# A hybrid attention network on one core: the attention's software pipeline made one step deeper

## The chip, the cores and the metric

The kernel runs on one core of one Trainium2 chip. The metric is the device time of one execution in microseconds (us), over the whole program. TensorE's engine is called PE, its weight loads PEld, VectorE is DVE, ScalarE is ACT, GpSimd is POOL, and SyncE, which issues most loads, is SP.

## What is computed

Two layers work on 512 tokens of width 1024. Each layer normalizes, projects, runs two kinds of attention side by side, projects back, and then runs a feed-forward part with a width-3 convolution. All is float32; the large products are made of three single-pass products of split operands.

```python
for l in range(2):
    proj = rms_norm(x, attn_norm[l]) @ w_in[l]
    q_lat, kv_lat, k_rope, nsa_q, nsa_kv, gate_logits = split(proj)
    o_mla = mla_attention(...)      # 8 heads, causal softmax over 512 keys
    o_nsa = nsa_attention(...)      # 8 heads in 2 groups; branches: compressed, selected, window
    x = x + concat([o_mla, o_nsa]) @ w_out[l]
    x = x + conv_ffn(rms_norm(x, ffn_norm[l]), ...)   # width 2816
out = rms_norm(x, final_norm)
```

At this length the selected branch (16 blocks of 64 tokens, of 8 that exist) and the window branch (512 tokens) are both plain causal attention with keys and values of their own. The compressed branch attends to 31 summaries, made by a small network from the first pair of keys and values.

## The kernel before, in words

Every engine has its own hand-written program, and semaphores tie them. There is no scheduler: what an engine does next is the order in its own list, and a wait holds everything behind it in that list.

**The attention of a layer** is one loop over 48 units (`U`, line 71) and a few steps for the pipeline to drain. A unit is one block of 128 queries of a pair of heads in one branch. Four units make a group `g` (12 groups: 4 of MLA, 8 of the other kind), in the order of `ORDER = (2, 3, 0, 1)` (line 74): causal units of 3, 4, 1 and 2 key blocks. Units of 3 and 4 blocks are "big" (line 606): each head takes a bank of PSUM of its own; the small ones put both heads into one bank. A unit passes through these stations:

- `scores(u)` (line 1620, PE): the products of queries and keys. MLA units use plain float32 (L1630), the others two products (L1635, L1636).
- `row_max(u)` (line 1191, DVE): adds the causal mask, writes the negated scores from PSUM into the tile `probs` and takes the row maximum (L1197).
- `exps(u)` (line 868, ACT): the exponential in place, with its row sum (L873).
- `turn(u)` (line 1639, PE): transposes the probabilities block by block into PSUM (L1649).
- `evac_turn(u)` (line 876, ACT): copies the transposed blocks to the tiles `pts` in SBUF (L884 and L887 for the two heads of a big unit, L891 for a small one).
- `values(u)` (line 1678, PE): for two units at once (odd u), the products with the values (L1696).
- per group: `factors(g)` (line 1200, DVE; L1203 and L1208 or L1212) makes one over the row sums, `spread(g)` (line 1654, PE; L1663) transposes them, `copy_factors(g)` (line 1220, DVE; L1223) brings them back, `normalize(g)` (line 1225, DVE; L1230, for every second later group also L1234) multiplies the output, `evac_out(g)` (line 895, ACT; L898, the first four groups only) and `out_lo` (line 1236, DVE; L1238) split it for the projection that follows.

**The loops.** PE, ACT and DVE each run over a step `s`. Before the change `LAG = 4` and `T_LAG = 3` (lines 72 and 73). In step s PE does turn(s-3), spread, scores(s), and values(s-4) on odd s, in that order. ACT does evac_turn(s-3), then exps(s). DVE does copy_factors, row_max(s), factors, normalize. Into this are hung single pieces of work at fixed steps (lines 108 to 116): projections in steps 0 to 2, eight "items" (transposes of queries and keys, `ITEM_STEP`, with `item_hi` on ACT and `item_lo` on DVE), the hidden layer of the compression (`HID_STEP` 7, L1731), its GELU over DVE, POOL, ACT and DVE again (L1315, L700 to L709, L941, L1321 to L1325), the product that needs it (`KVC_STEP` 11, L1835), the scores of the compressed branch and their softmax (steps 14 to 26), and four splits of output weights (`WOUT_STEP` 32, 36, 40, 44; L570 on ACT, L577 on DVE a step later).

**Banks.** PSUM has eight banks. Scores and spread factors go round banks 0 to 2, transposed probabilities round banks 3 and 4, and from step 29 on 3 to 5. The helper `ring` (line 125) hands out the bank that was used longest ago and names its former user; PE waits until that user has been read: `scores_read` (line 1605) for the row maxima or the copy of the factors on DVE, `turn_read` (line 1613) for the copies on ACT. The outputs of the first five groups share bank 6, so `out_free` (line 1667) makes values wait until the group before is normalized.

**Buffers.** `probs` (line 268) holds three units. row_max(u) may write only when turn(u-3) is done (line 1194). `pts` (line 269) are two tiles, each of four blocks, one for the units of 3 and 4 blocks and one for those of 1 and 2.

**After the loop's units** (s >= 48) PE fills its time with the first three parts of the output projection (`FILL = 3`, lines 1792 to 1799). The first of them waits for all row maxima, because it writes banks 0 to 3.

Of the kernel before, what the change touches and what calls it, by code (L numbers as in the profile page):

```python
# [32 lines left out]
P = 128  # L33
# [35 lines left out]
U_MLA = (H // 2) * T  # L69
U_NSA = (H // 2) * 2 * T  # L70
U = U_MLA + U_NSA
LAG = 4
T_LAG = 3
ORDER = (2, 3, 0, 1)


# [48 lines left out]
def ring(uses, banks):  # L125

    table, last = {}, {}
    for use, allowed in uses:
# [8 lines left out]
              (turn_uses(s) if s < U else [])]  # L137
TURN_USES = [(use, (3, 4) if s <= PC_STEP[1] + 2 else (3, 4, 5) if s < U else (4, 5)) for s in range(T_LAG, U + LAG)
             for use in (turn_uses(s - T_LAG) if s < U + T_LAG else []) +
             ([("f", NG - 1)] if s == U + LAG - 1 else [])]  # L140
SCORE_BANK = ring(SCORE_USES, 3)
TURN_BANK = ring(TURN_USES, 3)
FAC_BANK = [(TURN_BANK if g == NG - 1 else SCORE_BANK)["f", g] for g in range(NG)]
LAST_TURN_ON_3 = [use for use, _ in TURN_USES if TURN_BANK[use][0] == 3][-1]


# [23 lines left out]
def at(s, l, n):  # L170

    return l * PER_LAYER[s.name] + (n + CREDIT.get(s.name, 0))
# [74 lines left out]
def hybrid_layers(nc, a, out):  # L247

    with ExitStack() as ctx:
        def sb(name, shape, dt=F32, scope=ctx):  # L250
            return scope.enter_context(nc.sbuf_tensor(name, shape, dt))
# [13 lines left out]
        w_hi = sb("w_hi", [P, SLOTS, 1024], F32R)  # L265
        w_lo = sb("w_lo", [P, SLOTS, 1024], F32R)

        probs = sb("probs", [P, 3, 2, S])
        pts = [sb(f"probs_t{n}", [P, 2, T, 2 * P]) for n in range(2)]
        ident = sb("ident", [P, P])  # L270
        causal = sb("causal", [P, S])
        table = sb("table", [P, S])
# [43 lines left out]
        silu = sb("silu", [P, 2, S], F32, ffn)  # L316
        ffn.close()

        kpe_r = pts[1][:, 0, :, 0:2 * ROPE].rearrange("p t (a b) -> p t a b", a=2)
        rows = pts[0][:, 0, :, :].rearrange("p a (b c) -> p (a b) c", c=P)  # L320
        hn = probs[:, 0:2, :, :].rearrange("p s a n -> p s (a n)")
        norm_g = probs[:, 2, :, :].rearrange("p a n -> p (a n)")
# [425 lines left out]
        def _(act):  # L748
# [30 lines left out]
            for l in range(L):  # L779
# [88 lines left out]
                def exps(u):  # L868
                    n = (unit(u)[0] + 1) * P
                    for h in range(2):  # L870
                        row = probs[:, u % 3, h, 0:n]
                        act.wait_ge(max_done, at(max_done, l, 2 * u + h + 1))
                        activate(row, row, ACT.Exp, scale=-1.0, bias=nmax[:, u % 4, h:h + 1],  # L873
                                 accum_out=rsum[:, u // T % 2, unit(u)[0], h:h + 1]).then_inc(exp_done, 1)
# [43 lines left out]

                for s in range(U + LAG + 2):
                    if s < len(STEP_PROJ):  # L920
                        for job in STEP_PROJ[s]:
                            evac_proj(*job)
                    if 0 <= s - T_LAG < U:
                        evac_turn(s - T_LAG)
                    if s < U:
                        exps(s)
                    if s == 2:
                        act.wait_ge(gate_in, at(gate_in, l, 1))
                        activate(gates[:, :, :], gate_e[:, :, :], ACT.Exp, scale=-1.0).then_inc(gate_exp, 1)
                    g = (s - LAG - 1) // T  # L930
                    if s > LAG and (s - LAG - 1) % T == T - 1:
                        if g < H // 2:
                            evac_out(g)
                    if s in ITEM_STEP:
                        item_hi(ITEM_STEP.index(s))
                    if s == HID_STEP:
                        act.wait_ge(cmp_used, at(cmp_used, l, 4))
                        activate(hid_rows, ps[:, HID_BANK, 0:CHID], ACT.Copy).then_inc(hid_out, 1)
                    if s == HIDT_STEP + 1:
                        act.wait_ge(gelu_in, at(gelu_in, l, 1))  # L940
                        activate(gelu_t, gelu_t, ACT.Exp, scale=-2.0 * (2.0 / np.pi) ** 0.5).then_inc(gelu_exp, 1)  # L941
                    if s == KVC_STEP:
                        act.wait_ge(kvc_acc, at(kvc_acc, l, 1))
                        activate(kc[:, :, :], ps[:, KVC_BANK, S - G * NCP:S].rearrange("p (g c) -> p g c", g=G), ACT.Copy)\
                            .then_inc(kch_done, 1)
                    if s in CS_STEP:
                        g = CS_STEP.index(s)
                        act.wait_ge(cs_acc, at(cs_acc, l, g + 1))
                        activate(cs_t[g], ps[:, CS_BANK[g], :], ACT.Copy).then_inc(cs_out, 1)
                    if s in CS_EXP_STEP:  # L950
                        g = CS_EXP_STEP.index(s)
                        act.wait_ge(cs_sub, at(cs_sub, l, g + 1))
                        activate(sc_flat[g], sc_flat[g], ACT.Exp).then_inc(cs_exp, 1)
                    if s in PC_STEP:
                        g = PC_STEP.index(s)
                        act.wait_ge(pc_tp, at(pc_tp, l, g + 1))
                        activate(pct[:, g, :], ps[:, PC_BANK, :], ACT.Copy).then_inc(pct_ready, 1)
                    if s in WOUT_STEP:
                        split_hi(act, l, POS_WOUT + WOUT_STEP.index(s))
# [82 lines left out]
        def _(dve):  # L1042
# [47 lines left out]
            for l in range(L):  # L1090
# [99 lines left out]

                def row_max(u):
                    n = (unit(u)[0] + 1) * P
                    if u >= 3:
                        dve.wait_ge(t_done, at(t_done, l, turns(u - 3, 1 if big(u - 3) else 0)))
                    for h in range(2):
                        dve.wait_ge(sc_done, at(sc_done, l, 2 * u + (h + 1 if big(u) else 2)))
                        v.tensor_tensor_reduce(probs[:, u % 3, h, 0:n], score_place(u, h), causal[:, S - n:S], -1.0, -NEG,  # L1197
                                               ALU.add, ALU.min, nmax[:, u % 4, h:h + 1]).then_inc(max_done, 1)

                def factors(g):  # L1200
# [85 lines left out]
                for s in range(U + LAG + 2):  # L1286
# [5 lines left out]
                        add_compressed((s - LAG - 1 - U_MLA) // (2 * T))  # L1292
                    if LAG <= s < U + LAG and (s - LAG) % T == T - 1:
                        copy_factors((s - LAG) // T)
                    if s < U:
                        row_max(s)
                    if s < len(STEP_PROJ):
                        for job in STEP_PROJ[s]:
                            evac_proj(*job)
                    if 0 <= s - 2 < U and (s - 2) % T == T - 1:  # L1300
                        factors((s - 2) // T)
                    if s > LAG and (s - LAG - 1) % T == T - 1:
                        normalize((s - LAG - 1) // T)
                    if closed and done >= H // 2 and done % 2 == 1:
# [143 lines left out]
        def _(pe):  # L1448
# [30 lines left out]
            for l in range(L):  # L1479
# [132 lines left out]

                def turn_read(use):

                    if use is not None and use[1] == 0:
                        pe.wait_ge(pt_act, at(pt_act, l, use[0] + 1))
                    elif use is not None:
                        pe.wait_ge(pt_second, at(pt_second, l, pt_second_count(use[0])))
# [20 lines left out]
                def turn(u):  # L1639
                    blocks = unit(u)[0] + 1  # L1640
                    for h in range(2):
                        pe.wait_ge(exp_done, at(exp_done, l, 2 * u + h + 1))
                        if h == 0 or big(u):
                            turn_read(TURN_BANK[u, h][1])
                        bank, c0 = (TURN_BANK[u, h][0], 0) if big(u) else (TURN_BANK[u, 0][0], h * blocks * P)
                        if bank == PC_BANK and TURN_BANK[u, h if big(u) else 0][1] is None:
                            pe.wait_ge(pct_ready, at(pct_ready, l, G))
                        for b in range(blocks):
                            last = nc.tensor.transpose(ps[:, bank, c0 + b * P:c0 + (b + 1) * P],  # L1649
                                                       probs[:, u % 3, h, b * P:(b + 1) * P], ident[:, :])  # L1650
                        if h == 1 or big(u):
                            last.then_inc(t_done, 1)

                def spread(g):

                    pe.wait_ge(fac_ready, at(fac_ready, l, g + 1))
                    bank, prev = FAC_BANK[g]
                    if g == NG - 1:
                        turn_read(prev)
                    else:  # L1660
                        scores_read(prev)
                    for i in range(T):
                        last = nc.tensor.transpose(ps[:, bank, i * P:(i + 1) * P], onorm[:, g % 2, i * P:(i + 1) * P],  # L1663
                                                   ident[:, :])
                    last.then_inc(fac_done, 1)
# [85 lines left out]
                for s in range(U + LAG):  # L1751
# [35 lines left out]
                        pe.wait_ge(k_ready, at(k_ready, l, H // 2))  # L1787
                    if s >= LAG + U_MLA and (s - LAG - U_MLA) % (2 * T) == 2 * T - 1:
                        compressed((s - LAG - U_MLA) // (2 * T))
                    if s >= LAG and s % 2 == 1:  # L1790
                        values(s - LAG)
                    if s >= U and s - U < FILL:
                        pe.wait_ge(max_done, at(max_done, l, 2 * U))
                        if s == U:
                            pe.wait_ge(fac_out, at(fac_out, l, NG - 1))
                            turn_read(LAST_TURN_ON_3)
                        pe.wait_ge(lo_done, split(l, POS_WOUT + s - U))
                        for t in range(2):
                            project_out(t, s - U, [ht_hi[:, s - U, :], ht_lo[:, s - U, :]], s == U, False)
                    if s == T_LAG:  # L1800
                        pe.wait_ge(q_ready, at(q_ready, l, H))
                    if s == ITEM_STEP[0]:
                        pe.wait_ge(q_roped, at(q_roped, l, 1))
# [197 lines left out]
```

## Time and profile before

| | us |
|---|---|
| median of 3 runs | 1308.6 (1306.14 to 1309.12) |
| the profiled execution | 1306.81 |
| its span, first to last instruction | 1305.0 |
| PE busy in the span | 1263.9 (97%) |
| DVE busy | 700.7 (54%) |
| ACT busy | 639.0 (49%) |
| POOL busy | 71.3 (5%) |
| mean granted TensorE clock | 0.997 |

The span leaves out 1.8 us that lie around it. The attention loop of layer 0 runs from about 101.7 us to 251.7 us of the span, that of layer 1 from about 744 to 894. A row of the timeline gives the start, the duration, the engine and line, the tiles written and read, and in brackets how long the engine sat idle before it and what ended that. A row of a waits view gives the waiting engine and line, the one that released it, the sum in us, the number of times and the longest. PE's rows overlap: a matmul's record lasts longer than the distance to the next one's start, so the cost of a piece of PE work is read from start to start.

### The profile page before, as it was taken

The numbers are of one execution on the slowest core, as the hardware profiler recorded it, in microseconds if no ns is written. First come the engines' busy times: TensorE is split into PE (matmuls) and PEld (weight loads), VectorE is DVE, ScalarE is ACT, GpSimd is POOL, SyncE is SP. The second block draws the span as 40 slices with busy tenths as digits, with TensorE's granted clock in tenths as the row PEclk, the third lists the DMA queues.
The fourth block names the chain that finished last, engine by engine and source line by source line (L and its number), as shares of the span: only waits on it lengthen the run. The fifth ranks groups of instructions, "written<-read, shape, count | busy, mean of one in ns | idle before, by whom it ended". The sixth has DMA issues, their size and how long they took to land.

```text
span 1305.0 us, 18503 instructions
## 1 busy us (share of the span) xinstructions
PE 1263.9 (97%) x6612; PEld 1044.6 (80%) x6612; DVE 700.7 (54%) x1226; ACT 639.0 (49%) x1193; POOL 71.3 (5%) x165
## 2 busy tenths in 40 slices
PE   8999989999999999999999998999999999999997
PEld 7997667778888888888889866767888888888886
DVE  5435788454555555533363458872555555554334
ACT  4436789344444444322352468882454444443223
POOL 2003120000000000000010311100000000000000
PEclk9999999999999999999999999999999999999999
DMA  6420101124333333322143210022223333333211
GB/s 206 125 89 1 66 2 49 50 67 126 96 96 97 96 95 98 110 95 96 44 122 95 65 66 1 2 66 81 81 77 97 96 96 97 96 102 111 96 64 65
DMA packets 121003, 107.05 MB, mean 82 GB/s; under 512 B 3763, under 2 KB 110485, under 8 KB 120946
## 3 DMA queue, kind: packets, MB, share of 16 engines
q1 hardware_dynamic: 118912, 101.13, 25.2%
q0 software_dynamic: 1456, 3.52, 0.9%
q10 hardware_dynamic: 578, 1.64, 0.3%
q8 instruction: 35, 0.57, 0.2%
q14 instruction: 22, 0.18, 0.0%
HBM read 104.19 MB, written 2.10 MB: 81 GB/s over the span
## 4 chain that ended last, share of the span: by engine, by line
PE 84%; DVE 9%; ACT 4%; issue 2%; DMA 1%; POOL 0%; DVEq 0%; ACTq 0%; POOLq 0%
PE ps L1453 24%; PE ps L1455 24%; PE ps L1454 24%; PE ps L1649 3%; PE ps L1696 3%; DVE probs L1197 2%; PE ps L1630 2%; ACT probs L873 1%; DVE probs L1070 1%; DVE w_lo L577 1%; PE ps L1636 1%; PE ps L1635 1%; DVE x L1088 1%; PE ps L1708 1%; PE ps L1663 1%
## 5 line engine op out<-in xcount | busy, mean ns | idle before, releaser
L1453 PE MATMUL ps<-ht_hi,w_hi 128*128 128x512 f32 (+2 forms) x776 | 298.0, 384 | 2.5 <-DVE w_lo L577 2.5
L1454 PE MATMUL ps<-ht_lo,w_hi 128*128 128x512 f32 (+2 forms) x776 | 296.4, 382 | 0.0
L1455 PE MATMUL ps<-ht_hi,w_lo 128*128 128x512 f32 (+2 forms) x776 | 296.4, 382 | 0.0
L577 DVE TENSOR_TENSOR w_lo<-raw,w_hi 128x1024 fp32r<-128x1024 f32 (+4 forms) x196 | 218.6, 1140 | 95.9 <-ACT w_hi L570 86.3
L570 ACT ACTIVATE w_hi<-raw 128x1024 fp32r<-128x1024 f32 (+4 forms) x196 | 187.2, 983 | 108.3 <-PE ps L1455 107.1
L1369 DVE SCALAR_TENSOR_TENSOR conv<-ps,cols,conv 128x510 f32<-128x510 f32 (+1 forms) x176 | 127.6, 745 | 181.5 <-ACT conv L982 175.6
L1453 PEld LDWEIGHTS ps<-ht_hi,w_hi 128*128 128x128 f32 x776 | 146.4, 189 | 30.9 <-DVE w_lo L577 2.9
L1454 PEld LDWEIGHTS ps<-ht_lo,w_hi 128*128 128x128 f32 x776 | 146.4, 189 | 28.2 <-issue 0.5
L1455 PEld LDWEIGHTS ps<-ht_hi,w_lo 128*128 128x128 f32 x776 | 146.3, 189 | 27.7
L1453 PE MATMUL ps<-w_hi,ht_hi 128*128 128x430 f32 (+1 forms) x392 | 147.0, 375 | 3.3 <-DVE w_lo L577 2.0
L982 ACT ACTIVATE conv<-ps,cols 128x512 f32<-128x512 f32 x88 | 68.1, 774 | 160.0 <-PE ps L1455 159.7
L1455 PE MATMUL ps<-w_hi,ht_lo 128*128 128x430 f32 (+1 forms) x392 | 144.2, 368 | 0.0
L1454 PE MATMUL ps<-w_lo,ht_hi 128*128 128x430 f32 (+1 forms) x392 | 144.2, 368 | 0.0
L1453 PE MATMUL ps<-w_hi,g_hi 128*128 128x512 f32 x352 | 137.2, 390 | 0.8 <-DVE g_all L1377 0.8
L1454 PE MATMUL ps<-w_lo,g_hi 128*128 128x512 f32 x352 | 137.0, 389 | 0.0
L1455 PE MATMUL ps<-w_hi,g_lo 128*128 128x512 f32 x352 | 136.9, 389 | 0.0
L873 ACT ACTIVATE probs<-probs,nmax 128x384 f32<-128x384 f32 (+1 forms) x192 | 106.2, 557 | 30.2 <-DVE nmax L1197 29.7
L1197 DVE CUSTOM_DVE_ANT_0 probs<-ps,causal 128x384 f32<-128x384 f32 (+1 forms) x192 | 86.8, 486 | 42.7 <-PE ps L1630 22.5
L1001 ACT ACTIVATE g_hi<-g_all 128x512 fp32r (+1 forms) x44 | 27.6, 630 | 149.8 <-PE ps L1455 149.8
L1390 DVE TENSOR_TENSOR g_lo<-g_all,g_hi 128x512 fp32r<-128x512 f32 x44 | 30.2, 691 | 129.8 <-ACT g_hi L1001 129.8
L1649 PE MATMUL ps<-ident,probs 128*128 128x128 f32 x480 | 72.1, 278 | 17.7 <-ACT probs_t L891 9.7
L1453 PEld LDWEIGHTS ps<-w_hi,ht_hi 128*128 128x128 f32 x392 | 73.8, 188 | 11.7 <-DVE w_lo L577 2.6
(201 smaller groups left out, 1506.4 us busy)
## 6 DMA issues: line engine op xcount, KB each, us to landing
raw<-in_ffn_w_up_dram SPq DMA_DIRECT2D x88, 512.0 KB, 4.2
raw<-in_ffn_w_down_dram SPq DMA_DIRECT2D x44, 512.0 KB, 3.3
raw<-in_w_in_dram SPq DMA_DIRECT2D x32, 430.0 KB, 4.2
raw<-in_w_out_dram SPq DMA_DIRECT2D x16, 512.0 KB, 3.3
raw<-in_nsa_cmp_w_dram SPq DMA_DIRECT2D x8, 512.0 KB, 3.6
x<-in_x_dram ACTq DMA_DIRECT2D x3, 512.0 KB, 8.2
raw<-in_mla_w_uq_dram SPq DMA_DIRECT2D x4, 384.0 KB, 3.0
out_dram<-x SPq DMA_DIRECT2D x3, 512.0 KB, 2.6
```

Source lines behind the costliest of these rows:

```text
L570: last = nc.scalar.activation(d(w_hi)[:, :, d0:d1], r(raw)[:, :, r0:r1], ACT.Copy)
L577: last = nc.vector.tensor_tensor(d(w_lo)[:, :, d0:d1], r(raw)[:, :, r0:r1], d(w_hi)[:, :, d0:d1].bitcast(F32), ALU.subtract)
L873: activate(row, row, ACT.Exp, scale=-1.0, bias=nmax[:, u % 4, h:h + 1], accum_out=rsum[:, u // T % 2, unit(u)[0], h:h + 1]).then_inc(exp_d ...
L982: activate(conv[:, fl, uv, :], ps[:, 4 * fl + uv, :], ACT.Identity, bias=bias, scale=tap)\
L1197: v.tensor_tensor_reduce(probs[:, u % 3, h, 0:n], score_place(u, h), causal[:, S - n:S], -1.0, -NEG, ALU.add, ALU.min, nmax[:, u % 4, h:h ...
L1369: ins = stt(out=conv[:, fl, uv, back:S], in0=ps[:, 4 * fl + uv, 0:S - back], scalar=c, in1=conv[:, fl, uv, back:S], op0=ALU.mult, op1=ALU.add)
L1390: tt(g_lo[:, n % 2, :].unsqueeze(1), g_all[:, bass.ds(k, 1), :], g_hi[:, n % 2, :].unsqueeze(1).bitcast(F32), ALU.subtract).then_inc(gl_do ...
L1453: mm(o, lhs[0], rhs[0], start=start, stop=False)
L1454: mm(o, lhs[0], rhs[1], start=False, stop=False)
L1455: return mm(o, lhs[1], rhs[0], start=False, stop=stop)
L1649: last = nc.tensor.transpose(ps[:, bank, c0 + b * P:c0 + (b + 1) * P], probs[:, u % 3, h, b * P:(b + 1) * P], ident[:, :])
L1696: last = mm(ps[64 * h:64 * h + VD, out_bank(g), q0 + q:q0 + 2 * P], w, pt_half(u)[:, h, b, q:2 * P], start=b == 0, stop=b == n - 1)
```

## The change

`LAG` becomes 5 and `T_LAG` 4. `probs` gets a fourth buffer; the second tile of `pts`, which serves the units of 1 and 2 blocks only, shrinks to two blocks. In step s PE now does turn(s-4), spread, scores(s), and values(s-5) on even s. ACT does evac_turn(s-4) and then exps(s-1). On DVE `factors` moves from one step after the group's last exponentials were issued to the head of the step behind, ahead of row_max; copy_factors and normalize follow one step later than before. The single pieces of work stay at their steps. The spread of group 10 falls to step 48, so that it takes a bank of the transposes' ring. The wait for all queries goes from step `T_LAG` to the first item's step, which is again step 3.

```diff
-LAG = 4
-T_LAG = 3
+LAG = 5
+T_LAG = 4
...
-             ([("f", NG - 1)] if s == U + LAG - 1 else [])]
+             ([("f", (s - LAG) // T)] if s >= U and (s - LAG) % T == T - 1 else [])]
...
-FAC_BANK = [(TURN_BANK if g == NG - 1 else SCORE_BANK)["f", g] for g in range(NG)]
+FAC_BANK = [(SCORE_BANK if ("f", g) in SCORE_BANK else TURN_BANK)["f", g] for g in range(NG)]
...
-        probs = sb("probs", [P, 3, 2, S])
-        pts = [sb(f"probs_t{n}", [P, 2, T, 2 * P]) for n in range(2)]
+        probs = sb("probs", [P, 4, 2, S])
+        pts = [sb(f"probs_t{n}", [P, 2, T // (n + 1), 2 * P]) for n in range(2)]
...
-                        row = probs[:, u % 3, h, 0:n]
+                        row = probs[:, u % 4, h, 0:n]
...
-                    if s < U:
-                        exps(s)
+                    if 1 <= s <= U:
+                        exps(s - 1)
...
-                    if u >= 3:
-                        dve.wait_ge(t_done, at(t_done, l, turns(u - 3, 1 if big(u - 3) else 0)))
+                    if u >= 4:
+                        dve.wait_ge(t_done, at(t_done, l, turns(u - 4, 1 if big(u - 4) else 0)))
...
+                    if 0 <= s - 3 < U and (s - 3) % T == T - 1:
+                        factors((s - 3) // T)
                     if s < U:
                         row_max(s)
...
-                    if 0 <= s - 2 < U and (s - 2) % T == T - 1:
-                        factors((s - 2) // T)
...
-                    if use is not None and use[1] == 0:
+                    if use is not None and use[0] == "f":
+                        pe.wait_ge(fac_out, at(fac_out, l, use[1] + 1))
+                    elif use is not None and use[1] == 0:
...
-                    if g == NG - 1:
+                    if ("f", g) not in SCORE_BANK:
...
-                    if s >= LAG and s % 2 == 1:
+                    if s >= LAG and (s - LAG) % 2 == 1:
                         values(s - LAG)
...
-                            pe.wait_ge(fac_out, at(fac_out, l, NG - 1))
+                            pe.wait_ge(fac_out, at(fac_out, l, sum(("f", g) in SCORE_BANK for g in range(NG))))
...
-                    if s == T_LAG:
+                    if s == ITEM_STEP[0]:
                         pe.wait_ge(q_ready, at(q_ready, l, H))
```

## Rows read from the trace of the kernel before

**Rows 1.** The page's first part: busy time of each engine, share, instructions.
```profile
PE 1263.9 (97%) x6612; PEld 1044.6 (80%) x6612; DVE 700.7 (54%) x1226; ACT 639.0 (49%) x1193; POOL 71.3 (5%) x165
```

**Rows 2.** Windows: the two attention loops; length, busy time by engine, PE clock.
```profile
113.40:251.70 138.30, 127.62 (x968) 94.70 (x967) 98.29 (x290) 102.76 (x295) 12.83 (x17) 1.00 0.09 32
...
755.90:894.30 138.40, 127.74 (x968) 94.80 (x967) 98.34 (x290) 102.80 (x295) 12.88 (x17) 1.00 0.09 32
```

**Rows 3.** Waits of PE in the attention loop of layer 0, 113.4 to 251.7.
```profile
PE ps L1649 <- ACT probs_t L891: 4.8, 3, 2.4
PE ps L1649 <- ACT probs_t L884: 4.0, 5, 1.4
PE ps L1747 <- DVE ks L1249: 1.3, 1, 1.3
PE ps L1851 <- DVE qs L1251: 0.5, 1, 0.5
```

**Rows 4.** Waits of ACT in the same stretch: the exponentials.
```profile
ACT probs L873 <- DVE nmax L1197: 14.9, 21, 1.4
```

**Rows 5.** Timeline of PE: the longest wait of the late groups, turn(45).
```profile
234.89 1.06 PE L1649 MATMUL ps<-ident,probs 128*128 128x128 f32 x8 [1.39 <-ACT probs_t L884]
```

**Rows 6.** Timeline of PEld: the weight load ahead of the same wait.
```profile
234.86 0.85 PEld L1649 LDWEIGHTS ps<-ident,probs 128*128 128x128 f32 x8 [1.60 <-ACT probs L873]
```

**Rows 7.** Timeline of ACT at the start of the loop of layer 0.
```profile
105.18 1.28 ACT L873 ACT_TABLE_LOAD   x1
106.48 0.62 ACT L873 ACTIVATE probs<-probs,nmax 128x384 f32<-128x384 f32 x1
...
108.33 1.20 ACT L850 ACTIVATE km<-ps 64x512 f32<-64x512 f32 x2 [0.54 <-PE ps L1455]
```

**Rows 8.** Timelines of ACT, DVE and POOL, layer 0, steps 8 to 11.
```profile
134.93 0.61 ACT L898 ACTIVATE ht_hi<-onorm 128x512 fp32r<-128x512 f32 x1
...
138.16 0.47 DVE L1315 TENSOR_SCALAR hid<-ps,hid_b 128x62 f32<-128x62 f32 x2
...
139.55 1.39 DVE L1249 TENSOR_TENSOR ks<-ps,ks 64x512 fp32r<-64x512 f32 x2
...
140.46 0.54 POOL L709 TENSOR_SCALAR tmp_pool<-tmp_pool 128x128 f32<-128x128 f32 x1 [0.20 <-POOL tmp_pool L705]
...
142.34 0.95 DVE L1323 RECIPROCAL tmp_pool<-tmp_pool 128x128 f32<-128x128 f32 x1
...
143.33 0.29 DVE L1325 TENSOR_TENSOR hid<-hid,tmp_pool 128x128 f32<-128x128 f32 x1
```

**Rows 9.** Timeline of DVE in steps 45 and 46 of layer 0.
```profile
229.38 0.68 DVE L1197 CUSTOM_DVE_ANT_0 probs<-ps,causal 128x512 f32<-128x512 f32 x1
...
230.83 0.69 DVE L1212 TENSOR_TENSOR onorm<-fac,gates 128x512 f32<-128x512 f32 x1
...
232.04 1.22 DVE L577 TENSOR_TENSOR w_lo<-raw,w_hi 128x1024 fp32r<-128x1024 f32 x1
...
233.17 0.28 DVE L1197 CUSTOM_DVE_ANT_0 probs<-ps,causal 128x128 f32<-128x128 f32 x1
```

**Rows 10.** Timeline of PE: an MLA step, then one whole later group.
```profile
133.78 1.88 PE L1630 MATMUL ps<-km,qm 128*128 128x512 f32 x4
135.59 1.74 PE L1696 MATMUL ps<-probs_t,vm 128*64 128x256 f32 x16
...
196.01 0.84 PE L1649 MATMUL ps<-ident,probs 128*128 128x128 f32 x6
...
197.78 0.87 PE L1696 MATMUL ps<-probs_t,proj 128*64 128x256 f32 x8
198.58 1.09 PE L1649 MATMUL ps<-ident,probs 128*128 128x128 f32 x8
199.43 0.42 PE L1635 MATMUL ps<-ks,qs 128*128 128x384 f32 x1
...
204.02 0.84 PE L1649 MATMUL ps<-ident,probs 128*128 128x128 f32 x6
```

More of the change, by code:

```diff
@@ L317, in hybrid_layers @@
         ffn.close()
-        kpe_r = pts[1][:, 0, :, 0:2 * ROPE].rearrange("p t (a b) -> p t a b", a=2)
+        kpe_r = pts[1].rearrange("p a t c -> p (a t) c")[:, :, 0:2 * ROPE].rearrange("p t (a b) -> p t a b", a=2)
         rows = pts[0][:, 0, :, :].rearrange("p a (b c) -> p (a b) c", c=P)
@@ L1192, in row_max @@
                     n = (unit(u)[0] + 1) * P
-                    if u >= 3:
-                        dve.wait_ge(t_done, at(t_done, l, turns(u - 3, 1 if big(u - 3) else 0)))
+                    if u >= 4:
+                        dve.wait_ge(t_done, at(t_done, l, turns(u - 4, 1 if big(u - 4) else 0)))
                     for h in range(2):
                         dve.wait_ge(sc_done, at(sc_done, l, 2 * u + (h + 1 if big(u) else 2)))
-                        v.tensor_tensor_reduce(probs[:, u % 3, h, 0:n], score_place(u, h), causal[:, S - n:S], -1.0, -NEG,
+                        v.tensor_tensor_reduce(probs[:, u % 4, h, 0:n], score_place(u, h), causal[:, S - n:S], -1.0, -NEG,
                                                ALU.add, ALU.min, nmax[:, u % 4, h:h + 1]).then_inc(max_done, 1)
@@ L1649, in turn @@
                             last = nc.tensor.transpose(ps[:, bank, c0 + b * P:c0 + (b + 1) * P],
-                                                       probs[:, u % 3, h, b * P:(b + 1) * P], ident[:, :])
+                                                       probs[:, u % 4, h, b * P:(b + 1) * P], ident[:, :])
                         if h == 1 or big(u):
```

## The prediction, made before the changed kernel was run

> **What bounds the kernel now.** I began with the page's busy times: PE has work for 97% of the span [rows 1], so the whole time stands at most some tens of us above PE's own work. A change to the attention's order adds and removes no PE instruction, so it can only win or lose PE's waiting. The windows of the two attention loops say how much that is: 138.3 us with 127.62 busy, and 138.4 with 127.74 [rows 2], about 10.7 us idle in each. ACT is busy for 103 us there and DVE for 98, so neither is the bound over a whole loop, but a group can be. The waits view names what ended the idle time: 8.8 us by ACT's copies of transposed blocks (L891, L884), in 8 waits, and 1.8 by DVE, in two [rows 3]. The timeline shows the longest late one at turn(45), 1.39 us [rows 5]; its weight load waited 1.60 [rows 6], so each wait also costs 0.21 us of drain that still counts as busy. The ten waits are thus worth 10.6 + 10 x 0.21 = 12.7 us a layer, 25 us in all: the most that the change can win. Layer 1 shows the same ten.
>
> Why are ACT's copies late? In ACT's list evac_turn stands behind the exponentials of the step before, and these wait for a fresh row maximum: 14.9 us a layer in 21 waits for DVE [rows 4]. The deeper pipeline lets exps(s-1) run on maxima that are a step old. That wait should go almost wholly, and PE's eight waits for copies with it.
>
> **What is added, part by part.** Nothing is added in instructions: the same copies, exponentials, transposes and products, and no DMA (SP's loads hang on other steps; POOL's load after the loop waits for the last transpose, but stands behind its last copy, which comes later anyway). The fourth `probs` buffer is free of cost: no wait in the trace is for the old three. One more drain step has no work of its own; the copies of turn(47) are covered by spread and the compressed product. What costs is order. I follow each list through steps 3 to 52, one layer, with durations of the rows, a hand-over from PE to DVE of 0.3 and from ACT or DVE to PE of 0.1 to 0.15 us.
>
> *The start.* exps(0) moves behind the keys' copy of step 1, which ended at 109.53, and takes its table load (1.28) along [rows 7]; before, the load fell into idle time. From there ACT works without a gap (exps 0 to 2, keys, gates, item 0) and copies turn(0) at 117.2; its half is done at 117.64, and PE, which reaches turn(1) at 116.8, waits 1.0. In this case the load ends at 106.46 and the exponential starts at 106.48, with nothing behind it [rows 7], so I add nothing. The Trainium skill (ScalarE: Activation LUTs, "What ACT_TABLE_LOAD costs") puts a drain of about 1.38 us on top of each load; by it this wait would be 2.4 us and the whole 2.8 us slower than my sum. The trace speaks against it.
>
> *values behind normalize.* For groups 1 to 4 values wait until the group before is normalized. normalize used to follow a 3-block row_max; now it follows the 4-block one of step 4g+5, and values come on the next step, after just a 1-block turn and scores. In MLA, from scores(9)'s start: scores take 1.81 [rows 10], the second maximum starts 0.3 later and takes 0.69, normalize 0.69, ready for PE at 3.6; PE is there at 1.81 + 0.45 (item) + 0.22 + 0.45 = 2.9. Wait 0.5 to 0.6 for groups 1 and 2. In groups 3 and 4 the scores are shorter and no item covers: 0.8 and 1.1. Together 3.0.
>
> *GELU before KVC_STEP.* This is the largest. Count from the start of turn(5). scores(9) end at 2.7, normalize(0) at 4.4, DVE's hidden-layer pieces (L1315) at 5.1. ACT does evac_out (0.61) at 4.5 and item 2 (1.19) to 6.3. DVE does out_lo, factors and row_max(10) to 6.8 and item_lo(2), 1.39, to 8.2; then the GELU's three instructions, 0.94 + 0.95 + 0.29 with gaps, 2.25, to 10.4 [rows 8]. PE, without turn(8), spread(1) and values(7), which used to stand ahead of it, gets to KVC_STEP at 8.0. Wait 2.5, in place of the 2.4 [rows 3] that this same chain costs now through POOL (L709 [rows 8]) and ACT.
>
> *Scores behind a busy DVE.* Three banks and seven uses a group: the second half of scores(4k) now takes the bank of scores(4k-1), the step before, and needs its maximum. DVE's list in between, from the 4-block maximum: 1.21, normalize 0.69, in every second group a sum of the same shape (0.69), the weight split 1.13 (232.04 to 233.17), factors 0.85, the 1-block maximum 0.42, out_lo 0.6, the 2-block maximum 0.76: 6.4 us [rows 9]. It starts 0.8 behind scores(37). PE from there to the second half of scores(40): the group's 8.01 less values 0.80, turn 0.85 and half the 3-block scores 0.35, thus 6.0 [rows 10]. 0.8 + 6.4 + 0.15 - 6.0 = 1.3 wait at step 40. Without the sum and out_lo the list is 5.1 and fits; without the split (step 32) 0.2. At step 48 the same list holds back the output projection, which needs all maxima, and spread(10) needs a copy of turn(44) at once: 0.65. Together 2.2.
>
> *The rest*, found in the same way: item 6 behind item_lo(5) 0.4, turn(14) behind item 7 on ACT 0.3, turn(20) 0.7 and scores(24) 0.5 around the compressed softmax, turn(24) 0.15. Together 2.1.
>
> **The sum.** Added per layer 1.0 + 3.0 + 2.5 + 2.2 + 2.1 = 10.8; removed 12.7. Gain 1.9 a layer, 3.8 in all; I take 3.6, for small hand-overs. The profiled execution took 1306.81, so 1303.2; the median of the runs is 1.8 above it, so against that 1305.0. Bounds of the unknown waits: if the GELU chain and normalize are hidden by what PE does ahead of them, 2.5 + 3.0 less half, so 3 a layer, are not paid, gain 10. If each of the 14 new waits is 0.3 longer than worked out (as much as one hand-over to DVE), 4.2 a layer more are lost.
>
> **Rivals.** *The covers hold*: ACT's slack removes the waits and the new ones are half of mine; for it speaks that the removed 14.9 us of ACT's waiting [rows 4] exceed all of PE's. 1308.6 - 10 = 1298.6. *Nothing to be measured*: old and new waits cancel within 0.2%, about what a measurement of this kernel can tell from no change (2.6 us). The banks for transposes (two, later three) and scores (three) stay, and all of PE's waits for ACT are for a bank [rows 3]; only the `probs` buffer grows, which no wait names. If the bubbles are set by banks, the time stays 1308.6. The Trainium skill (Perfetto Trace Analysis, "Optimization Strategy") says that a gap that repeats on the engine that should be full can mean too little SBUF or PSUM for the next tile; by that rule this change gives room in the memory that isn't short. *Slower, by DVE*: the place is the step after the 4-block maximum, where normalize, split and factors now pile up (4.0 us between two maxima [rows 9], where factors, out_lo and split stood before), with PE waiting for it in values, KVC, items and scores(4k). It decides from the point where the added waits exceed 12.7 a layer, that is with 0.15 us more on each of 14. At 0.3 more each: (4.2 - 1.9) x 2 = 4.6 slower, 1313.2. Against it: I counted ready times from records of the same instructions.
>
> **How the numbers follow.** Forecast, a small gain around 1305.0: 0.42. Covers hold, 1298.6: 0.13. Nothing, 1308.6: 0.2. Slower by DVE, 1313: 0.25. Of the forecast 0.35 and of the covers all lies below 1306.0, so faster 0.48; same 0.07 + 0.2 = 0.27; slower 0.25. Both signs hold much of the chance: the forecast's own range is 1302 to 1308. The range for 8 in 10 reaches to both other cases, 1298 to 1313.
>
> **What would show it.** Right: PE's waits for L884 and L891 fall from 8.8 us a layer to under 3; ACT's wait for L1197 from 14.9 to under 4; new are a wait of 2 to 3 us at L1835 for L1325, waits at L1696 for L1230 in four groups, and at step 40 one at L1635 for L1197. Wrong: waits of L1649 for ACT still near 8 us (banks decide), or no wait at L1835, or waits for DVE above 11 us a layer. A granted clock under 1.00 in the loop would be outside all of this.

## The result, and the profile after

| | before | changed |
|---|---|---|
| median | 1307.49 us (6 runs) | 1315.71 us (6 runs, 1314.57 to 1317.45) |
| ratio | | 1.0063, 95% interval 1.0052 to 1.0073: slower |
| profiled execution | 1306.81, span 1305.0 | 1317.45, span 1315.6 |
| mean granted clock | 0.997 | 0.993 |

The forecast was 1305.0 with a range of 1298 to 1313. The change made the kernel slower where a gain was forecast, and the time lies outside the range. (The rows of after have the line numbers of the changed kernel: of the lines in PE's program that the text names, all but L1453 to L1455 are two higher.)

The page's first part answers to [rows 1]. PE was busy for 7.4 us longer, with the same 6612 instructions:

```profile
PE 1271.3 (97%) x6612; PEld 1050.5 (80%) x6612; DVE 704.6 (54%) x1226; ACT 638.3 (49%) x1193; POOL 78.3 (6%) x165
```

Next, windows from the first product of scores to the start of the last values, first in the kernel before, then in the changed one. Columns: the window, its length, busy time (and records) of PE, PEld, DVE, ACT, POOL, then the granted clock, the DMA share and GB/s.

```profile
101.69:248.17 146.48, 135.80 (x997) 100.65 (x995) 102.79 (x306) 111.04 (x311) 20.76 (x51) 1.00 0.09 30
744.24:890.70 146.46, 135.80 (x997) 100.66 (x995) 102.78 (x306) 111.02 (x311) 20.75 (x51) 1.00 0.09 30
```
```profile
102.03:254.16 152.13, 140.42 (x997) 104.26 (x995) 104.69 (x306) 110.67 (x311) 24.26 (x51) 0.98 0.08 29
750.67:902.82 152.15, 140.46 (x996) 104.27 (x994) 104.70 (x306) 110.67 (x311) 24.25 (x51) 0.98 0.09 29
...
143.40:146.80 3.40, 3.40 (x17) 2.79 (x14) 1.92 (x3) 2.85 (x12) 0.00 (x0) 0.52 0.00 0
...
239.00:242.40 3.40, 3.40 (x13) 2.54 (x10) 1.81 (x4) 0.17 (x2) 0.00 (x0) 0.52 0.02 7
791.90:795.30 3.40, 3.40 (x24) 2.81 (x13) 2.04 (x3) 2.98 (x12) 0.00 (x0) 0.53 0.00 0
887.50:890.90 3.40, 3.40 (x15) 2.42 (x12) 1.94 (x4) 0.30 (x2) 0.00 (x0) 0.53 0.00 0
```

Each loop is 5.65 to 5.69 us longer, and this is where the time went. Idle time (length less busy) rose only from 10.7 to 11.7. Busy time rose by 4.6, and the last four windows say why: twice in each loop the clock falls to half (1.2 in place of 2.4 GHz) for 3.4 us (the windows lie up to 0.2 us beside these stretches, so that they read 0.52 or 0.53). Before, the only such stretch ahead of the program's last few us was in the feed-forward part of layer 1 (936.2 to 939.6), and after the change that one is gone. The span's 10.6 us more are 11.3 in the loops, 0.3 ahead of the first, 0.4 between them, and 1.5 less behind the second (414.3 to 412.8).

The waits of PE from 100 to 250, layer 0, which answer to [rows 3], and ACT's wait, which answers to [rows 4]. Columns: who waits, for whom, us in total, times, the longest.

```profile
PE ps L1837 <- DVE hid L1325: 2.6, 1, 2.6
PE ps L1698 <- DVE onorm L1230: 2.6, 4, 1.1
PE ps L1637 <- DVE nmax L1197: 2.1, 3, 1.1
PE ps L1665 <- ACT probs_t L884: 2.0, 1, 2.0
PE ps L1651 <- ACT probs_t L884: 0.9, 2, 0.7
PE ps L1665 <- DVE onorm L1212: 0.6, 1, 0.6
PE ps L1720 <- DVE qs L1251: 0.5, 1, 0.5
PE ps L1651 <- ACT probs_t L891: 0.2, 1, 0.2
```
```profile
ACT probs L873 <- DVE nmax L1197: 3.5, 5, 1.3
```

ACT's 14.9 us of waiting for maxima fell to 3.5, as it should, and PE's waits for copies from 8.8 to 3.1. In their place stand waits for DVE, 8.4 us in ten where there had been 1.8 in two. All in all there are 14 waits, 11.5 us, where ten with 10.6 us had been. The two longest, on PE's timeline (start, duration, idle time before in brackets), and the matmuls behind the second:

```profile
142.66 0.41 PE L1837 MATMUL ps<-hid,cmp_w 128*128 128x64 f32 x2 [2.65 <-DVE hid L1325]
...
237.96 0.63 PE L1665 MATMUL ps<-ident,onorm 128*128 128x128 f32 x4 [2.02 <-ACT probs_t L884]
...
240.45 0.63 PE L1455 MATMUL ps<-w_hi,ht_lo 128*128 128x512 f32 x1
240.88 0.63 PE L1453 MATMUL ps<-w_hi,ht_hi 128*128 128x512 f32 x1
...
243.27 0.40 PE L1454 MATMUL ps<-w_lo,ht_hi 128*128 128x512 f32 x1
243.51 0.39 PE L1455 MATMUL ps<-w_hi,ht_lo 128*128 128x512 f32 x1
```

Each of the two is followed by one of the windows at half clock, in which products start 0.43 apart (240.45 to 240.88) in place of 0.24. Why is the second 2.02 long? DVE and ACT ahead of it:

```profile
232.69 0.69 DVE L1230 TENSOR_TENSOR onorm<-ps,onorm 128x512 f32<-128x512 f32 x1
233.48 0.69 DVE L1234 TENSOR_TENSOR onorm<-onorm 128x512 f32<-128x512 f32 x1
234.09 1.22 DVE L577 TENSOR_TENSOR w_lo<-raw,w_hi 128x1024 fp32r<-128x1024 f32 x1
...
235.45 0.87 DVE L1212 TENSOR_TENSOR onorm<-fac,gates 128x512 f32<-128x512 f32 x1
236.24 0.28 DVE L1197 CUSTOM_DVE_ANT_0 probs<-ps,causal 128x128 f32<-128x128 f32 x1
```
```profile
236.56 0.40 ACT L873 ACTIVATE probs<-probs,nmax 128x128 f32<-128x128 f32 x1 [1.29 <-DVE nmax L1197]
...
237.35 0.47 ACT L884 ACTIVATE probs_t<-ps 128x384 f32<-128x384 f32 x1
```

The pile of [rows 9] is there in its new order: maxima, normalize, sum, split, factors, maxima. exps(46) waits 1.29 for it, the copy of turn(44) stands behind exps(46) in ACT's list, and PE waits for the copy.

### The profile page after: what moved, and what is told of

The parts are those of the page before. It is cut to its first block, busy times and chain, and to the rows that moved or that the text cites. A ratio compares the mean times of both kernels' runs of the same rounds, so it can differ in the third digit from the quotient of the medians.

```text
span 1315.6 us, 18499 instructions
## 1 busy us (share of the span) xinstructions
PE 1271.3 (97%) x6612; PEld 1050.5 (80%) x6612; DVE 704.6 (54%) x1226; ACT 638.3 (49%) x1193; POOL 78.3 (6%) x165
## 4 chain that ended last, share of the span: by engine, by line
PE 86%; DVE 8%; ACT 3%; issue 2%; DMA 1%; POOL 1%; DVEq 0%; ACTq 0%; POOLq 0%
PE ps L1453 24%; PE ps L1454 24%; PE ps L1455 24%; PE ps L1651 3%; PE ps L1698 3%; PE ps L1632 2%; DVE probs L1197 1%; PE ps L1637 1%; PE ps L1638 1%; DVE w_lo L577 1%; DVE probs L1070 1%; DVE x L1088 1%; PE ps L1665 1%; DVE onorm L1230 1%; PE ps L1710 1%
## 5 line engine op out<-in xcount | busy, mean ns | idle before, releaser
L1453 PE MATMUL ps<-ht_hi,w_hi 128*128 128x512 f32 (+2 forms) x776 | 297.5, 383 | 2.5 <-DVE w_lo L577 2.5
L1455 PE MATMUL ps<-ht_hi,w_lo 128*128 128x512 f32 (+2 forms) x776 | 296.2, 382 | 0.0
L1453 PEld LDWEIGHTS ps<-ht_hi,w_hi 128*128 128x128 f32 x776 | 145.9, 188 | 30.9 <-DVE w_lo L577 2.9
L1455 PEld LDWEIGHTS ps<-ht_hi,w_lo 128*128 128x128 f32 x776 | 145.9, 188 | 28.0
L1454 PEld LDWEIGHTS ps<-ht_lo,w_hi 128*128 128x128 f32 x776 | 146.0, 188 | 27.7 <-issue 0.5
L1453 PE MATMUL ps<-w_hi,ht_hi 128*128 128x430 f32 (+1 forms) x392 | 148.5, 379 | 4.4 <-DVE ht_lo L1077 2.4
L1455 PE MATMUL ps<-w_hi,ht_lo 128*128 128x430 f32 (+1 forms) x392 | 145.4, 371 | 0.0
L1453 PE MATMUL ps<-w_hi,g_hi 128*128 128x512 f32 x352 | 137.3, 390 | 0.8 <-DVE g_all L1377 0.8
L1455 PE MATMUL ps<-w_hi,g_lo 128*128 128x512 f32 x352 | 137.1, 390 | 0.0
L1453 PEld LDWEIGHTS ps<-w_hi,ht_hi 128*128 128x128 f32 x392 | 74.7, 190 | 13.7 <-DVE ht_lo L1077 2.9
L1455 PEld LDWEIGHTS ps<-w_hi,ht_lo 128*128 128x128 f32 x392 | 74.4, 190 | 7.2
```

What stands on the lines that cost most here:

```text
L1453: mm(o, lhs[0], rhs[0], start=start, stop=False)
L1454: mm(o, lhs[0], rhs[1], start=False, stop=False)
L1455: return mm(o, lhs[1], rhs[0], start=False, stop=stop)
```

## Experiments

The theory: DVE's order makes PE's new waits, and the two long ones also cost clock. Twelve kernels bear on it. The table has every run: its ratio to the kernel before, the lengths of the two loops (first scores to last values), and the number of 3.4 us stretches at half clock in each (one of 6.8 counts as two). The last column is the first loop less 1.73 us for each such stretch: about the loop's length by its waits alone (where that price comes from, and that it can be up to 0.25 too high for a stretch, is under a4_split). Medians are of all executions of a kernel, loops and stretches those of the profiled one, and executions of one kernel differ in clock: a2_norm's profiled one took 1303.2 at a mean clock of 0.992, its other three 1298.5 to 1299.3 at 0.996 to 0.997.

| run | median | ratio (95% interval) | loops | half clock | at full clock |
|---|---|---|---|---|---|
| before | 1307.49 | 1 | 146.5 / 146.5 | 0 / 0 | 146.5 |
| changed | 1315.71 | 1.0063 (1.0052 to 1.0073) | 152.1 / 152.2 | 2 / 2 | 148.7 |
| a1_fill | 1320.70 | 1.0094 (1.0069 to 1.0118) | 153.2 / 153.2 | 0 / 0 | 153.2 |
| a2_norm | 1298.93 | 0.9927 (0.9903 to 0.9951) | 145.1 / 145.2 | 2 / 2 | 141.7 |
| a3_kvc | 1320.22 | 1.0089 (1.0064 to 1.0113) | 152.6 / 151.1 | 2 / 1 | 149.2 |
| a4_split | 1306.30 | 0.9988 (0.9976 to 1.0000) | 147.8 / 146.0 | 1 / 0 | 146.0 |
| a5_fill | 1312.81 | 1.0033 (1.0021 to 1.0044) | 149.4 / 149.3 | 0 / 0 | 149.4 |
| b1_exps | 1303.18 | 0.9956 (0.9943 to 0.9969) | 144.9 / 143.3 | 1 / 0 | 143.2 |
| c1_both | 1300.16 | 0.9934 (0.9921 to 0.9946) | 144.9 / 143.4 | 2 / 1 | 141.4 |
| c2_more | 1301.66 | 0.9950 (0.9939 to 0.9962) | 144.8 / 144.8 | 1 / 1 | 143.0 |
| d1_lag | 1331.15 | 1.0179 (1.0165 to 1.0192) | 159.3 / 159.0 | 3 / 3 | 154.1 |
| d2_hid | 1296.84 | 0.9909 (0.9895 to 0.9922) | 143.0 / 141.3 | 1 / 0 | 141.3 |
| d3_b1norm | 1295.22 | 0.9900 (0.9887 to 0.9914) | 141.1 / 141.1 | 0 / 0 | 141.1 |
| d4_warm | 1297.97 | 0.9914 (0.9899 to 0.9930) | 141.8 / 141.8 | 0 / 0 | 141.8 |

**The clock (a1_fill, a5_fill).** Dummy transposes ahead of the two long waits, once what they write may be written:

```diff
+                        turn_read(TURN_BANK[8, 0][1])
+                        junk(24)          # a1_fill: 44
                         pe.wait_ge(it_act, at(it_act, l, 3))
...
+                        turn_read(LAST_TURN_ON_3)
+                        junk(18)          # a1_fill: 36
```

> The changed kernel with TensorE kept at work in its two longest waits of a layer: 44 transposes of the identity into a bank that is free, just ahead of the product at KVC_STEP, and 36 ahead of spread(10). They add nothing to the result. Clock theory: the granted clock falls to half after these two waits, for 3.4 us each time, four times in all, and each costs some 1.6 us; then the clock stays at full speed in the loops, and the time falls by 5 to 7 us, to about 1309 to 1311. Rival, the waits alone make the loss and the low clock costs nothing since other engines are late anyway: time within 1 us of the changed kernel's 1315.7, whatever the clock does.

The half-clock stretches in the loops went, but each transpose takes 0.112 us: the 44 outlast the wait of 2.65 by some 2.3 us, the 36 theirs by 2. The time rose, which neither side had forecast, and it says nothing about the theory's sum. Sized to the waits:

> The changed kernel with 24 dummy transposes ahead of TensorE's wait for the hidden layer (2.65 us) and 18 ahead of its wait at the step 48 copy (2.02 us); at 0.112 us each they take 2.7 and 2.0 us, as long as the waits. Theory (each of these waits is followed by 3.4 us at half the clock, 1.7 us lost a time): the work arrives when it did, no stretch at half clock is left in the two loops, and the time is 5 to 7 us less than the changed kernel's 1315.7: 1309 to 1311. Rival (the clock costs nothing on the path, the queues behind make it up): within 1 us of 1315.7.

Measured 1312.8, some 3 us below the changed kernel (4 by the ratios): neither forecast. The loops lost 2.77 and 2.82 us. Counted from the first loop's start, the product at KVC_STEP came 0.5 later (41.13 in place of 40.63), since the filling could start only 0.46 after PE was there. From it to spread(10) PE gained 1.73 (93.57 in place of 95.30), from there to the last values 1.54 (14.66 in place of 16.20). One stretch appeared at 942.6 in the feed-forward part (some 1.6 us), where the changed kernel had none. So the clock is on the path: its two stretches cost 1.73 and 1.54, 3.3 us a layer. That the place of a stretch can shift out of the loop I had not counted.

**DVE's order (a2_norm, a4_split, c1_both).** normalize ahead of the step's maxima; the weight splits two steps later; both.

```diff
+                    if s > LAG and (s - LAG - 1) % T == T - 1:
+                        normalize((s - LAG - 1) // T)
                     if 0 <= s - 3 < U and (s - 3) % T == T - 1:
...
-                    if s > LAG and (s - LAG - 1) % T == T - 1:
-                        normalize((s - LAG - 1) // T)
...
-                    if s - 1 in WOUT_STEP:
-                        split_lo(dve, l, POS_WOUT + WOUT_STEP.index(s - 1))
+                    if s - 3 in WOUT_STEP:
+                        split_lo(dve, l, POS_WOUT + WOUT_STEP.index(s - 3))
```

> The changed kernel with normalize moved ahead of row_max in DVE's list, within the same step. Order theory: DVE had to pass the 4-block maximum before it could normalize, and values waited for it; the waits of L1698 for L1230 (2.6 us a layer and 0.2 of drain for each of four) go, the GELU chain starts 0.7 us earlier, and DVE's list before the last maxima is 0.7 to 1.4 us shorter: the time falls by 6 to 10 us, to 1306 to 1310. Rival, DVE is simply full and its order matters little: what values gain, row_max and scores lose, less than 2 us.

> The changed kernel with DVE's four splits of output weights two steps later, behind the 2-block maximum in place of the 4-block one. Order theory: the list between the 4-block and the 2-block maximum is 1.13 us shorter, so the waits at step 40 (0.60 and 0.67) go and the wait for turn(44)'s copy at step 48 (2.02) falls to about 0.9, and with it the low clock behind it: 2 x (1.3 + 1.1) to 2 x (1.3 + 1.1 + 1.6), 5 to 8 us less, 1308 to 1311. Rival, these waits hang on ACT's load alone: unchanged, within 1.5 us of 1315.7.

a2_norm, 1298.9, is faster than the kernel before, and 7 us under the best that its theory forecast. Its waits of PE, 100 to 250:

```profile
PE ps L1837 <- DVE hid L1325: 2.3, 1, 2.3
PE ps L1637 <- DVE nmax L1197: 1.3, 1, 1.3
PE ps L1651 <- ACT probs_t L884: 0.9, 2, 0.7
PE ps L1665 <- ACT probs_t L884: 0.6, 1, 0.6
PE ps L1651 <- ACT probs_t L891: 0.6, 1, 0.6
PE ps L1720 <- DVE qs L1251: 0.4, 1, 0.4
```

The four waits for normalize are gone, and with them those for maxima at steps 32 and 40, and 1.4 of the 2.02 at spread(10): 11.5 became 6.1. normalize had stood behind factors and the step's two maxima, and PE behind normalize. The loops are 7.0 us shorter with as many half-clock stretches as in the changed kernel: 5.4 of idle time, and seven waits fewer, of 0.21 of drain each.

a4_split, 1306.3, beat its theory's 1308 to 1311 too, and it gives the clock's price. Its two loops have the same waits (9.5 us against 9.4), and its windows:

```profile
102.07:249.83 147.76, 138.20 (x997) 102.88 (x995) 104.47 (x306) 110.35 (x311) 23.74 (x51) 0.99 0.09 30
745.87:891.90 146.03, 136.50 (x996) 101.88 (x994) 104.44 (x306) 110.36 (x311) 23.73 (x51) 1.00 0.09 30
143.80:147.20 3.40, 3.40 (x13) 2.33 (x11) 2.02 (x4) 2.40 (x11) 0.00 (x0) 0.53 0.00 0
```

The first loop has one stretch at half clock, the second none: 1.73 us. Of the other runs in which the two loops differ by one stretch, d2_hid gives 1.71, b1_exps 1.60, c1_both 1.52 and a3_kvc 1.48, so the price is 1.5 to 1.7. The Trainium skill (TensorE: Matmul & The Clock Gate, "HAM oscillation — how this bites in real kernels") charges throttled time with one half of its length. That is 1.7 for 3.4, and the traces agree for the dearest stretches; the cheapest cost 0.2 less. The wait at spread(10) fell from 2.02 to 0.7, and no half clock followed it.

> The changed kernel with two orders on VectorE: a group's normalisation ahead of the step's maxima, and the weight splits two steps later. Theory (the waits for the normalisation and for the copy at step 48 are separate orders of VectorE's queue, and their effects add): waits behind the normalisation none, at the step 48 copy under 0.7, time 1293 to 1297. Rival (they are one and the same backlog, seen twice): no better than the first alone, 1298 to 1300.

The rival held: 1300.2 is no better than a2_norm, and at full clock the loop is 141.4 against 141.7. The wait at spread(10) stayed 0.6. It was one backlog, seen at two places.

**The wait for the hidden layer (a3_kvc, c2_more, d2_hid, d4_warm).** First, PE asks a step later (KVC_STEP 12; DVE's reader of that bank moved to the head of its step).

> The changed kernel with the product that needs the GELU (KVC_STEP) at step 12 in place of 11 and DVE's copy of it at the head of step 13. Order theory: the wait of 2.65 us falls under 0.7, the low clock behind it goes with it: (2 + 1.6) x 2 = about 7 us less, 1309. Rival, DVE's queue of item_lo and GELU sets the end there, and the wait moves to items or transposes behind it: less than 3 us gained.

The rival held. The wait at KVC_STEP is gone, and PE waits 2.6 at turn(8) instead. The time even rose, to 1320.2: half clock came up in both feed-forward parts (from 301.3 and from 949.8), and went in one place of the loops only. Waits of PE, 100 to 250:

```profile
PE ps L1651 <- ACT probs_t L891: 3.4, 3, 2.6
```

ACT's copy stands behind ACT's own step in the GELU (L941), which waits for POOL: 1.71 us, here and in the changed kernel. Asking later does not help an engine whose next wait is for the same queue. Second, on top of c1_both, the hidden layer's pieces (L1315) at the head of DVE's step 9, in c2_more with the compressed scaling one step later too (`CS_SCALE_STEP` 23, 25).

> As the one before, and the hidden layer's pieces of VectorE at the head of its step 9, and the compressed cache's scaling a few steps later. Theory: TensorE's wait for the hidden layer falls from 2.3 to about 0.5 us, that for the maxima from 1.3 to under 0.5, and with them both stretches at half clock of each layer go: 1284 to 1292. Rival (the wait moves to the copies and maxima that now stand behind the pieces, as it did when the step was only put later): within 2 us of the run before.

> The run with both orders on VectorE, and VectorE's work on the hidden layer at the head of its step 9, but the compressed cache's scaling where it was. Theory (the late scaling is what made the two new waits for GpSimd's operands, 1.9 and 1.2 us, in the run that had both): those two waits are gone, the wait for the hidden layer is 1.7 us and that for the maxima 1.3 as before, and the time is 1297 to 1300. Rival (the earlier hidden layer itself pushes the operands back): the two waits stay, 1301 to 1303.

c2_more was no better than c1_both (within the rival's 2 us): the wait for the hidden layer fell to 1.7 and that for maxima went, but two came in. Waits of PE in c2_more, 100 to 256:

```profile
PE ps L1870 <- POOL v_operand L731: 1.9, 1, 1.9
...
PE ps L1870 <- POOL k_operand L731: 1.2, 1, 1.2
```

d2_hid without the late scaling has neither, at 1296.8. Its gain over c1_both is clock: at full clock the loops are alike (141.3 and 141.4), but it has one half-clock stretch where c1_both has three. Third, c1_both with 20 dummy transposes (2.2 us) in the wait of 2.3:

> The run with both orders on VectorE, and 20 dummy transposes (2.2 us at 0.112 us each) ahead of TensorE's wait for the hidden layer (2.3 us). Theory (the wait costs its own length and 1.73 us of clock behind it): the first stretch at half clock of each layer goes and the time falls by 2 x 1.7 us to 1296 to 1297.5. Rival (the clock falls anyway behind the later wait of 1.3 us, or in the next stage): 1299 or more.

1298.0, between the two. All three stretches of the loops went, the second of layer 0 too, though the wait of 1.3 us ahead of it was still there. One came up at 289.9 in the feed-forward part; the loops fell by 3.0 and 1.5, and 1.6 was given back there.

**The parts of the change (b1_exps, d1_lag, d3_b1norm).** b1_exps is the kernel before with one edit, d1_lag the changed kernel with the same edit undone:

```diff
-                    if s < U:
-                        exps(s)
+                    if 1 <= s <= U:
+                        exps(s - 1)
```

(The fourth buffer is no part of b1_exps.) d3_b1norm is b1_exps with DVE's two orders.

> The kernel before with one part of the change alone: the exponentials of a step issued behind the copies of that step, factors and values where they were, three buffers. Theory (this shift is the useful part: ScalarE's 14.9 us of waits for maxima a layer go, and with them the copies' lateness; the one-step shift of the values is what put the normalisations behind VectorE's long step): 1297 to 1303. Rival (the exponentials come too late for turns that were not moved, so TensorE waits there instead): 1307 or more.

> The changed kernel with one part undone: the exponentials of a step again behind the copies of that same step, the rest (fourth buffer, turns, values and factors a step later) as changed. Theory (the exponentials' shift is what took ScalarE's waits for maxima away; the deeper pipeline alone only moves the values behind VectorE's long step): ScalarE waits again some 10 to 15 us a layer for maxima, TensorE's waits for copies come back in part, and the waits for the normalisation stay: 1316 to 1324, slower than the changed kernel or equal to it. Rival (the turns, one step later, no longer feel a late exponential, and the exponentials' shift is what makes the copies late): faster than the changed kernel, 1308 to 1313.

Both theories held in their signs, the first at the edge of its range, the second beyond it: 1331.2 where 1316 to 1324 was forecast, with 24.0 us of ACT's waiting for maxima where it was 10 to 15. The exponentials' shift alone gives 1303.2: ACT has no wait for maxima left from 100 to 250, and PE's waits for copies are 3.9 us. The rest of the change alone (turns, values and factors moved, one more buffer) gives 1331.2, some 23 us slower than before; which of these parts costs how much was not tried. The waits in d1_lag, 101 to 262 (the last row: ACT, 100 to 256):

```profile
PE ps L1651 <- ACT probs_t L891: 6.3, 3, 2.6
PE ps L1837 <- DVE hid L1325: 2.9, 1, 2.9
PE ps L1651 <- ACT probs_t L884: 2.1, 3, 1.0
PE ps L1698 <- DVE onorm L1230: 1.9, 3, 1.1
PE ps L1698 <- ACT probs_t L884: 1.5, 2, 0.8
```
```profile
ACT probs L873 <- DVE nmax L1197: 24.0, 25, 2.8
```

PE's waits for copies are at the level of before (8.4 for the turns), and the waits for DVE came on top.

> The kernel before with the exponentials' shift and the same two orders on VectorE as in the run with both, so without the one-step shift of turns, values and factors. Theory (the deeper pipeline is worth what it takes from the waits for copies, some 1 to 2 us a layer, once nothing on VectorE is in its way): 1301 to 1303, slower than the same orders on the deeper pipeline (1300). Rival (the deeper pipeline gives nothing at all): 1297 to 1299.

The rival held, and more: 1295.2 is the fastest of all, 1% under the kernel before, with clock 0.999. Once DVE's order is right, the deeper pipeline buys nothing: without it the loops are 141.1 and 141.1, and those of c1_both at full clock 141.4 and 141.6. c1_both's two loops are 6.0 us longer together, and its three stretches are some 5 of that. Waits of PE in d3_b1norm, 100 to 256:

```profile
PE ps L1649 <- ACT probs_t L891: 2.4, 2, 1.5
PE ps L1747 <- DVE ks L1249: 0.9, 1, 0.9
PE ps L1635 <- DVE nmax L1197: 0.8, 2, 0.4
PE ps L1649 <- ACT probs_t L884: 0.7, 2, 0.6
PE ps L1708 <- ACT vm L957: 0.2, 1, 0.2
```

The orders of DVE without the exponentials' shift were not tried on the kernel before.

## Why the prediction was wrong

**What bounds the kernel** held: PE's waits, 25 us in all, and nothing else to win; the best kernel won 13 of them. **What the change removes** held in part. ACT's wait for maxima fell to 3.5 (forecast: under 4), PE's waits for copies to 3.1 (under 3, so just missed). These 3.1 are waits that the sum had among the added ones: 0.74 at turn(1), 0.41 at turn(14) and turn(20), and 2.02 ahead of spread(10).

**The added waits** were found at their places; only turn(24) showed none. Per layer, forecast and idle time measured: start and turn(1) 1.0 and 0.7; values behind normalize 3.0 and 2.6; KVC_STEP 2.5 and 2.65; scores at steps 32 and 40 1.5 and 1.65; the rest 2.1 and 2.0; step 48 0.65 and 2.02. Two terms of the sum failed:

- *Step 48, sized 1.4 too small.* "spread(10) needs a copy of turn(44) at once" was priced by the pile of DVE alone. The copy stands behind exps(46) on ACT, and exps(46) behind the pile: DVE's lateness was handed on through ACT's list. The text named the pile and the copy, and never put them in one chain.
- *The drain.* The old waits were credited with 0.21 each on top of the idle time, the new ones were not charged it. Like with like it is 11.5 + 14 x 0.21 = 14.4 against 12.7: waits alone cost 1.7 us a layer where I gained 1.9.

One term came out right by luck. The GELU's three instructions were priced 0.94 + 0.95 + 0.29, as in [rows 8], and took 0.23 + 0.95 + 1.11. The last one ran beside a cast on POOL:

```profile
141.30 1.11 DVE L1325 TENSOR_TENSOR hid<-hid,tmp_pool 128x128 f32<-128x128 f32 x1
```
```profile
140.10 2.17 POOL L717 CAST ks<-ks 64x1024 fp32r<-64x1024 f32 x2 [0.42 <-DVE ks L1249]
```

The forecast never asked what POOL does beside DVE. The 0.8 us that L1325 took longer lie in PE's wait of 2.65.

**The clock** is the step that failed altogether. The sum took each wait at its own length; "a granted clock under 1.00 in the loop would be outside all of this" named it and gave it no price and no chance. Two stretches a layer cost 3.3 of the 5.65 us (a5_fill). What causes the remaining 0.6 (5.65 less 1.7 and 3.3) is not shown. Forecast and result differ by 7.5 us a layer in the loops: 3.6 by waits, 3.3 by clock, 0.6 by the rest; the kernel before's own stretch, gone in the feed-forward part, gave 1.5 back once. With the waits counted right and no loss of clock the change would have come out some 4 us slower; with the clock it left the range.

**The rivals.** *Slower, by DVE* (1313.2, chance 0.25) is what happened, with its place, its turning point of 12.7 a layer and nearly its price in waits (14.4; it had 15.0); the clock made up the difference. *Nothing, since banks decide*, did not hold: with no bank added, PE's waits for copies fell by more than half in b1_exps (8.8 to 3.9) and in the changed kernel. The Trainium skill (Perfetto Trace Analysis, "Optimization Strategy") says of repeated gaps that they can mean too little SBUF or PSUM. That was not so here: order in two queues made these gaps. *The covers hold* did not happen; only a part of the change, b1_exps, made the kernel faster. *The table load:* turn(1) waited 0.74, not 2.4, and in the changed kernel too the load's end at 111.17 is 0.01 ahead of the exponential:

```profile
109.89 1.28 ACT L873 ACT_TABLE_LOAD   x1
111.18 0.62 ACT L873 ACTIVATE probs<-probs,nmax 128x384 f32<-128x384 f32 x1
```

So the drain of about 1.38 us (the Trainium skill, ScalarE: Activation LUTs, "What ACT_TABLE_LOAD costs") did not show here either.

## What to carry to other kernels

A change that shifts several stations by a step is several changes: price each alone, since here the exponentials' shift won 5 us and the deeper pipeline it came with lost 12 to 14 beside it, and 23 without it. Where a pipeline's engines run hand-written lists, first ask whether the order in a list is right; putting a 0.69 us instruction ahead of one that need not come first was worth 17 us to the changed kernel (14 between the two profiled executions, which had as many half-clock stretches). And do not price a wait of TensorE by its length alone: look in the profile for the clock around the waits that are already there, and give a loss of clock a price and a chance.

## What the runs showed of the hardware that was not expected

A stretch at half clock lasted 3.4 us (6.8 in d1_lag, behind waits of 2.62 and 0.68 close together) and cost 1.5 to 1.7 us in stages where PE was full. It followed waits of 2.65 and 2.02 us in the changed kernel and one of 1.3 in a2_norm; none followed 1.60 in the kernel before, 1.12 in the changed kernel or 0.7 in a4_split. The wait's length does not decide alone. In the kernel before PE waited 2.36 at 142.10 and kept its clock; in b1_exps the same wait of 2.36, to 141.91, had a stretch at half clock from 141.7 on, so the clock fell within the wait. Two loops of one execution with the same waits differed in it (a3_kvc, a4_split, b1_exps, c1_both, d2_hid). At the start of the feed-forward part, where PE waits 0.2, 0.8 and 1.2 us, stretches came and went with edits elsewhere (a1_fill, a3_kvc, a5_fill, b1_exps, c2_more, d4_warm). What decides where it falls stays open; runs of these kernels should be compared loop by loop, with the stretches counted.

DVE's product that ends the GELU (L1325) took 0.29 us with POOL idle (the kernel before and b1_exps, both layers) and 1.11 to 1.17 us in both layers of the other twelve kernels. There it started 0.02 to 0.07 us after POOL's second cast of L717 had started, and ended 0.14 to 0.15 after the cast's end. In the kernel before and b1_exps it was L1321 that started 0.17 to 0.18 after the first cast did, and it took 0.94 in place of 0.23 us. No run took the casts away, so what this is worth on PE's path is not shown.
